# Merge's gate and branch products as eight pieces of one product instead of four of two

## The reference, cut to what matters

```python
def merge_branches(ya, yb, yc, gate_logits, w_branch, w_out):
    ys = jnp.einsum('btiw,iwd->btid', jnp.stack([ya, yb, yc], axis=2), w_branch)
    gates = jax.nn.sigmoid(gate_logits.reshape(B, T, N_BRANCH, D_MODEL))
    return jnp.einsum('btd,de->bte', jnp.sum(gates * ys, axis=2), w_out)
```

## Time and profile before

| | |
|---|---|
| time, median of 3 runs | 2516.83 us (2514.77 to 2518.96) |
| the profiled execution's own time | 2520.44 us |
| its span, first to last instruction | 2518.6 us |
| mean granted PE clock | 0.938 of full |
| PE busy | 2239.4 us, 89%, 11226 matmul instructions |
| DVE, ACT, POOL busy | 956.4 us, 807.5 us, 352.4 us |
| DMA | 203.84 MB, mean 81 GB/s |

### The profile page before, as it was taken

The page is one execution under the profiler, slowest core; times in us unless marked ns, Lnnn a source line. Parts: engine busy times, 40 slices in busy tenths (PEclk is TensorE's granted clock), DMA queues, the critical chain, the costliest instruction groups (busy, mean ns, idle before and its releaser), DMA issues. The chain is left out here.

```text
span 2518.6 us, 32151 instructions
## 1 busy us (share of the span) xinstructions
PE 2239.4 (89%) x11226; PEld 1505.6 (60%) x11226; DVE 956.4 (38%) x2389; ACT 807.5 (32%) x2165; POOL 352.4 (14%) x568
## 2 busy tenths in 40 slices
PE   7998988697977989999999999988697876989998
PEld 3676555554554677555574447765464654866687
DVE  2023354555554334333231111235555553343321
ACT  2223242324332224444231122334324332234421
POOL 1000006060515000000000010001560633000000
PEclk8999999798988999999999999999697987999999
DMA  8214330221212112011222342113222222232243
GB/s 287 84 34 151 103 88 21 87 65 47 80 47 72 43 59 77 27 40 56 75 84 67 117 139 69 51 35 105 72 72 60 81 63 70 65 107 74 97 134 134
DMA packets 224735, 203.84 MB, mean 81 GB/s; under 512 B 29999, under 2 KB 220035, under 8 KB 224067
## 3 DMA queue, kind: packets, MB, share of 16 engines
q1 hardware_dynamic: 220608, 187.93, 24.3%
q0 software_dynamic: 2400, 13.52, 1.5%
q10 hardware_dynamic: 1571, 0.34, 0.1%
HBM read 184.91 MB, written 16.85 MB: 80 GB/s over the span
## 5 line engine op out<-in xcount | busy, mean ns | idle before, releaser
L1043 PE MATMUL bank<-hT,ring 128*128 128x512 f32 (+2 forms) x1856 | 725.3, 539 | 16.8 <-ACT WORK L1587 8.1
L1043 PEld LDWEIGHTS bank<-hT,ring 128*128 128x128 f32 (+1 forms) x1856 | 334.1, 191 | 275.2 <-issue 237.7
L1043 PE MATMUL bank<-ring,hT 128*128 128x256 f32 (+2 forms) x2112 | 465.5, 376 | 29.4 <-DMA ring<-in_w_in_dram 17.3
L1043 PEld LDWEIGHTS bank<-ring,hT 128*128 128x128 f32 x2112 | 390.3, 195 | 101.2 <-issue 30.8
L1043 PE MATMUL bank<-WORK 128*128 128x128 f32 (+5 forms) x2160 | 376.1, 325 | 45.6 <-issue 14.7
L1043 PEld LDWEIGHTS bank<-WORK 128*128 128x128 f32 (+2 forms) x2160 | 302.4, 197 | 152.9 <-issue 119.3
L1043 PE MATMUL bank<-yT,ring 128*128 128x512 f32 (+1 forms) x768 | 277.8, 496 | 0.0
L1043 PEld LDWEIGHTS bank<-yT,ring 128*128 128x128 f32 x768 | 140.6, 194 | 83.1 <-issue 74.2
L1012 POOL TENSOR_TENSOR WORK<-WORK 64x31 f32<-64x31 f32 (+15 forms) x248 | 150.9, 608 | 19.4
L1010 POOL TENSOR_TENSOR WORK<-WORK 64x31 f32<-64x31 f32 (+15 forms) x248 | 146.6, 591 | 19.4
L1948 DVE SCALAR_TENSOR_TENSOR WORK<-WORK,CW 128x512 f32<-128x512 f32 (+1 forms) x192 | 146.5, 763 | 3.3
(11 more groups left out here) (195 smaller groups left out, 2203.7 us busy)
## 6 DMA issues: line engine op xcount, KB each, us to landing
ring<-in_w_in_dram SPq DMA_DIRECT2D x92, 1024.0 KB, 5.5
ring<-in_ada_w_dram SPq DMA_DIRECT2D x24, 1024.0 KB, 6.2
ring<-in_w_branch_dram SPq DMA_DIRECT2D x24, 1024.0 KB, 5.1
LD<-WORK SPq DMA_DIRECT2D x64, 128.0 KB, 2.0
ring<-in_w_out_dram SPq DMA_DIRECT2D x8, 1024.0 KB, 4.9
ring<-in_mla_q_up_dram SPq DMA_DIRECT2D x8, 576.0 KB, 4.0
xs<-yT POOLq DMA_DIRECT2D x2, 2048.0 KB, 10.6
O<-XD SPq DMA_DIRECT2D x32, 128.0 KB, 2.5
```

The costliest lines, as they stand in the source:

```text
L1043: return nc.tensor.matmul(o, a, b, start=start, stop=stop, skip_group_check=True)
```

## The change

The number of pieces of the kinds `gate` and `ys` is 8 instead of 4, so that each piece is one product (two PE instructions). Nothing else is edited. The rest follows from the list:

```diff
-NPIECE = {"gate": 4, "ys": 4, "z": 4, "mod": 4, "dqkv": 4, "gqk": 4, "gv": 4, "lr": 4, "norm": 8}
+NPIECE = {"gate": 8, "ys": 8, "z": 4, "mod": 4, "dqkv": 4, "gqk": 4, "gv": 4, "lr": 4, "norm": 8}
```

## The result

The changed kernel takes 2527.87 us (median of 5, 2524.41 to 2528.93), against 2518.96 us (median of 5, 2514.77 to 2523.55) for the kernel before: a ratio of 1.0032, 95% interval 1.0017 to 1.0048. That is slower by more than the 0.2% which the text above takes for the resolution, and 0.9 us above the upper end of the predicted range. A second measurement gives 2525.19 us and a ratio of 1.0028 (1.0016 to 1.0039). The profiled execution has a span of 2527.1 us, 8.5 above the one before; its mean granted clock is 0.932, not 0.938.

A forecast was written before the change was run, and what follows sets the result against it. PE is busy 89% of the span, idle mostly on DVE's block inversions, ring loads and ACT's copies. Terms -0.5 -0.5 +0 +3.7 +0.7 -2.0 sum to +1.4 us, so a median of 2518.2 us; range 2509 to 2527 (8 in 10).

The forecast's parts named there:

- (c): Solve of group 3: earlier start against three more products ahead of PE's last d2; value 0, bounds -0.9 and +1.3 us.
- (a): Scans: su's waits behind st go (-1.6 us), other waits grow up to +1.1; layer 1 nothing; sum -0.5 us.
- (b): Second bank for dqkv 3: bank waits go but come back as a wait on O; -0.5 us, bounds -3.7 and 0.
- (d): z and low-rank stage, layer 0: longer ring wait and lower clock, partly given back at z2 waits; +3.7 us, bounds 0 and +7.
- (e): z and low-rank stage, layer 1: wait of 3.08 grows, mqT's 1.86 moves to mkT; +0.7 us, bounds -1.9 and +1.5.
- (f): Attention: waits on ACT's or DVE's last step change by a product; about -1 us per layer, -2.0, bounds -4 and +3.
- The slower rival: z stage, layer 0: the z product waits for its ring unit and nothing is given back; +7.3 us, 2524.1 us, chance 0.31.

The follow-up runs named there:

- B: The kernel before the change, the base of all ratios: 2518.96 us (median of 5).
- B's shares, single products: Against the changed kernel: each head, scan and inversion gets the same products of merge(l,0) as in B, still single within each place; ratio to B 1.0011.

## Why the prediction was wrong

The forecast was +1.4 us, the measured change +7.1 to +8.1 by the two ratios. That the first measurement lies 0.9 us outside the range and the second inside it matters little; the mechanism of the forecast was not the one that made the time. Two things made it slower than forecast: step (c), and the inversion of group 3, which has no step. By its steps:

- **(a), half right.** su's wait of 0.73 in group 3 is gone and the one in group 2 is at 0.18. The one in group 0 is still 0.88 (at 533.71), though a product of ys now lies between st and su: a product in between is not enough. The new wait ahead of sa is 0.88 at 664.63 (the text had up to +1.1), and su of group 1 has one of 0.40. All waits in the scans of layer 0 together go from 3.1 to 2.3 us: the -0.5 is near, but by other terms than these. That the scans of layer 1 come to nothing holds too.
- **(b), right for layer 0, half right for layer 1.** The gain of the second bank is given back: in layer 0 the way to group 2's first dx is 2.2 us shorter and that to the third 2.1 longer, and the experiment with one bank shows no difference. What the step did not see is that in layer 1 the clock falls there. I took "given back" for the worst case and set the upper bound at 0; but the bank is not what exceeds it, since the clock falls with one bank too.
- **(c), the step that failed.** It put three more products of ys and gate ahead of PE's last d2 and costed them at "0.86 + 0.43 = +1.3". Three products are 2.6 in layer 0 and 1.3 in layer 1, 3.9 in all: a slip of one product for three. Measured, from the third dx of group 2 to the last d2 of head 3: +2.8 and +2.2 (mean of three kernels with the change's order against four with B's). In layer 0 it is hidden, for the solve's other inputs had been later than PE (the way from the last d2 to the first dx shrinks by 2.5); in layer 1 only 0.6 is, so +1.7 where the text had 0. And I counted what was added to head 3 but not what was thereby taken from scan 1. The value 0 stood for all of this; undoing the cut, with the DVE entry back at its place, is worth 4.8 us by the timed runs.
- **(d), right in every wait.** 8.14 for 8.4, 1.84 for 2.0, 1.19 for 1.2. For the foretold net of +3.7, the stage from the first z piece to the first scores takes 3.1 us longer in the first profile of the change and 7.6 in the second (where mq(0,0) is at the low clock); the timed kernels with and without the ring wait differ by 2.3. The extra price of the clock, +0.7, can't be told from 0.
- **(e), right.** The wait of 3.08 is 3.26; mqT's 1.86 is gone.
- **(f), sign right, size too small.** Layer 1's attention gives 4.1 us, not 1. Layer 0's gives 3.7, not 1: from the first scores to the last mo 231.0 us before and 227.3 after, in both profiles, with PE's idle time down from 5.9 to 4.4 in the first.
- **Missing: the inversion of group 3.** No step of the sum touched it, for the waits in it did not change. It costs 3.6 us to the third dx in layer 1 (one product more, 0.43 at full clock, and for the rest the clock), and 5.5 by the timed runs. The earlier trace rows held the hint: 7.5 us at 0.57 behind the wait of 11.79, in the very stretch where the change puts single products between small steps. I used that row to price a wait elsewhere and did not ask what the change does to the stretch itself.

The slower rival had nearly the measured time, 2524.1, but for another reason: its test, that the waits at 985 and 1002 keep 2.43 and 2.94, came out against it. That its number was near is luck.

## What to carry to other kernels

When work is cut finer, look first at every place that counts entries: a share by number of entries moves work between stages as soon as an entry's size changes. In a loop that waits for a chain on another engine, filler belongs into the stretch that covers the chain and not ahead of what starts it, and if PE comes out of a long wait at half clock, try its large products together there: that gave 3.4 us at one place here (layer 1) and nothing at the like place in layer 0. A version that took the finer pieces only where PE waits for short steps of ACT and DVE (the attention) gained 0.2%, where using them everywhere lost 0.3%.

## What was not expected of the hardware

- In the two profiles of the change PE is busy for 8.6 and 14.9 us more than before, for the same instructions, with an equal and a smaller sum of idle time: the clock can make the whole of a change.
- PE's clock, low behind a wait of 16 to 19 us, rose 4.2 us behind it where products stood in twos and 10.8 us behind it where they stood singly among small steps, with no idle time over 0.2 us in that time.
- Behind a wait of 3.2 to 5.0 us mq(0,0) took 5.5 us in three profiles (waits of 3.25 to 3.44) and 6.9 to 8.5 in the ten others: the fall of the clock behind a wait of this length is not certain. And it fell in one profile (B's shares, single products) with no idle time over 1.08 us ahead.
- The page counts 288 instructions more (32439 against 32151) with the pieces of one product, all of them of PE's sequencer, so a piece boundary holds no matmul but is not empty, as the prediction had it; they cost nothing that a ratio of 1.0007 (0.9998 to 1.0016) would show.
